# Where packing and spreading lie among the weight quads of an expert pair

## The reference

```python
def hier_moe(h, w_rg, b_rg, w_re, b_re, w_gate, w_up, w_down):
    ...
    gates = jnp.einsum('tk,tke->te', weight, jax.nn.one_hot(expert_id, N_EXPERTS, dtype=jnp.float32))
    y = jnp.zeros(hf.shape, jnp.float32)
    for e in range(N_EXPERTS):
        a = jax.nn.silu(hf @ w_gate[e]) * (hf @ w_up[e])
        y = y + gates[:, e:e + 1] * (a @ w_down[e])
```

## Time and profile before

| | |
|---|---|
| timed runs, median (lowest to highest) | 1892.45 us (1890.16 to 1892.65) |
| profiled execution | 1889.55 us |
| its span | 1887.5 us |
| mean granted TensorE clock | 0.963 |
| TensorE busy | 1793.5 us, 95% |
| VectorE, ScalarE busy | 506.8 us, 300.8 us |
| ring loads | 168 of 2 MB, median 9.1 us from issue to landing |

### The profile page before, as it was taken

One profiled execution on the slowest core, in us unless ns is written; L12 is line 12 of the kernel. 1 busy time (PEld: TensorE's weight loads), 2 busy tenths in 40 slices (PEclk: granted clock), 3 DMA queues, 4 the chain that ended last, 5 costly groups with the idle time before them and its releaser, 6 DMA issues.

```text
span 1887.5 us, 18695 instructions
## 1 busy us (share of the span) xinstructions
PE 1793.5 (95%) x7908; PEld 1127.3 (60%) x7908; DVE 506.8 (27%) x1066; ACT 300.8 (16%) x666; POOL 31.9 (2%) x34
## 2 busy tenths in 40 slices
PE   7999999999999899999899999999999998999996
PEld 5776676577666654444367666766667666544442
DVE  0027653441110311121200185534211013111122
ACT  2114220130120210001111142102211102100101
POOL 0000000000100000000000000000010000000000
PEclk9999999799999799999999999999999997999998
DMA  6323215553264279999813322255423551999992
GB/s 270 129 94 134 93 45 200 201 200 134 89 223 178 90 280 391 356 386 369 357 61 118 139 88 90 94 200 219 178 90 134 214 187 58 400 361 390 360 386 122
DMA packets 28681, 382.68 MB, mean 203 GB/s; under 512 B 3184, under 2 KB 3568, under 8 KB 3888
## 3 DMA queue, kind: packets, MB, share of 16 engines
q1 hardware_dynamic: 25040, 356.69, 48.9%
q0 software_dynamic: 3552, 24.71, 3.2%
HBM read 356.67 MB, written 24.71 MB: 202 GB/s over the span
## 4 chain that ended last, share of the span: by engine, by line
PE 87%; DVE 4%; ACT 4%; DVEq 2%; issue 1%; DMA 1%; ACTq 0%; POOL 0%; SPq 0%; POOLq 0%
PE psum L472 29%; PE psum L925 12%; PE psum L750 7%; PE psum L945 6%; PE psum L910 5%; PE psum L970 4%; PE psum L809 3%; PE psum L839 3%; PE psum L713 2%; PE psum L690 2%; PE psum L710 2%; DVE work L1455 2%; PE psum L700 2%; PE psum L479 1%; PE psum L877 1%
## 5 line engine op out<-in xcount | busy, mean ns | idle before, releaser
L472 PE MATMUL psum<-h,ring 128*128 128x320 f32 x1920 | 533.7, 438 | 7.7 <-DVE h L1380 6.3
L472 PEld LDWEIGHTS psum<-h,ring 128*128 128x128 f32 x1920 | 366.8, 192 | 164.9 <-issue 17.3
L925 PE MATMUL psum<-ring,work 128*64 128x512 f32 x1024 | 231.9, 597 | 1.6 <-ACT work L1325 1.4
L925 PEld LDWEIGHTS psum<-ring,work 128*64 128x64 f32 x1024 | 69.6, 137 | 137.3 <-issue 132.5
L750 PE MATMUL psum<-work,ring 128*128 128x320 f32 x512 | 138.3, 433 | 0.9 <-ACT work L1100 0.9
L472 PE MATMUL psum<-mem,ring 128*128 128x256 f32 x512 | 123.0, 395 | 4.0 <-ACT work L1100 4.0
L750 PEld LDWEIGHTS psum<-work,ring 128*128 128x128 f32 x512 | 97.1, 190 | 42.0 <-ACT work L1100 1.8
L945 PE MATMUL psum<-ring,work 128*64 128x512 f32 x512 | 115.1, 603 | 7.2 <-ACT work L1340 7.2
L472 PEld LDWEIGHTS psum<-mem,ring 128*128 128x128 f32 x512 | 98.5, 197 | 21.2 <-issue 7.1
L910 PEld LDWEIGHTS psum<-work 128*128 128x128 f32 x768 | 92.1, 199 | 25.0 <-issue 22.7
L910 PE MATMUL psum<-work 128*128 128x128 f32 x768 | 97.8, 286 | 1.4 <-ACT work L1313 1.4
(11 more groups left out here) (242 smaller groups left out, 1467.0 us busy)
## 6 DMA issues: line engine op xcount, KB each, us to landing
ring<-stream SPq DMA_DIRECT2D x168, 2048.0 KB, 9.1
st_out<-states_out POOLq DMA_DIRECT2D x18, 1024.0 KB, 9.2
mk_out<-k_mem POOLq DMA_DIRECT2D x2, 1024.0 KB, 6.1
mv_out<-work POOLq DMA_DIRECT2D x2, 1024.0 KB, 5.6
cst<-consts SPq DMA_DIRECT2D x1, 1456.0 KB, 22.3
x<-x_in SPq DMA_DIRECT2D x1, 1280.0 KB, 5.7
y_out<-h POOLq DMA_DIRECT2D x2, 640.0 KB, 3.2
mem<-mem_in SPq DMA_DIRECT2D x1, 1024.0 KB, 24.2
```

The source lines that it names most:

```text
L472: mm = pe.matmul(out, w[:, a:a + P], rhs[:, j, :], start=(j == 0), stop=(j == KD - 1))
L925: mm = pe.matmul(psum[ab * CAP:(ab + 1) * CAP, up, :], h_packed[:, p % 2, k, ab * CAP:(ab + 1) * CAP], w[:, a:a + BANK], start=(k == 0), s ...
```

## The change

The two fillers of the gate/up quads change places. Before, quads 0 and 1 were each followed by half of the spreading of pair p - 1, and quads 2 and 3 each by half of the packing of pair p + 1. After, quads 0 and 1 are followed by the packing, quads 2 and 3 by the spreading. Nothing else is changed; the programs of VectorE, ScalarE and SP stay as they are.

```diff
                     for m in range(4):
                         gate_up(p, m)
-                        if m < 2 and p > 0:
-                            spread(p - 1, range(4 * m, 4 * m + 4))
-                        if m >= 2 and p + 1 < PAIRS:
-                            pack(p + 1, m - 2)
+                        if m < 2 and p + 1 < PAIRS:
+                            pack(p + 1, m)
+                        if m >= 2 and p > 0:
+                            spread(p - 1, range(4 * m - 8, 4 * m - 4))
                     pe.wait_ge(s_hid, n_p + 1)
```

## The result

The changed kernel takes 1920.96 us (median, 1914.2 to 1923.73), the kernel before 1891.31 in the runs beside it: 1.0159 of before, 95% interval 1.0121 to 1.0197. The forecast was 1928.3 with a range from 1908 to 1948, so direction and range hold. The time was forecast 7 us too long. The growth was forecast at 38.7 us and measured at 29.7; the difference is smaller in the time because the forecast started from a profiled execution of 1889.55, which is 1.8 us under the median of before. The profiled execution took 1918.65 us, with a span of 1916.7 against 1887.5.

The account below looks back on a forecast made before the run. Expert stage paced by the order of matmuls, DMA queue close behind. 20.0 (chain) + 2.8 + 1.2 + 8.8 (ring) + 5.9 (clock) = +38.7 us on the profiled 1889.55 gave 1928.3 us, range 1908 to 1948.

Parts of the forecast that it names:

- chain, pairs 1 to 6: Between fourth quad and down, the multiplication waits for the last four adds: +1.42 us a pair, +17.0 for 12 pairs.
- chain, pair 0: Pair 0 has nothing to spread, so nothing follows its fourth quad before down: +1.65 us, twice +3.3.
- chain, pair 7: Pair 7's uncovered time before down goes from 2.81 to 2.64 us: -0.17, twice -0.3.
- ring, quads 0 and 1 in pairs 1 to 6: Late slot release delays weight loads: quad 0 waits add +2.8 us (0 to 17), quad 1 waits +1.2 (0 to 4).
- ring, pair 7: Without packing behind quads 0 and 1, loads of quads 1 and 2 come 2.9 and 1.5 us late: +8.8 (2 to 12).
- clock: TensorE's clock falls to 1.2 GHz behind 4.5 passages instead of 1, lengthening down by 1.69 us each: +5.9 us.
- The passage: From the fourth gate/up quad's end to down's start in pairs 1 to 6: 5.30 us instead of 4.11.
- The ring as pace (no change): Rival: weight loads set the pace at 0.94 busy, a longer chain costs nothing, time stays near 1890 us; chance 0.05.
- The faster case: Rival: SiLU, multiplication and transposes hide under the spreading, some -8 us, 1882 us; chance 0.03.
- The clock in most passages: Rival: the clock falls in most passages before down, say 12 times, +18.6 instead of +5.9, 1938 us; chance 0.12.
- loads late everywhere: Rival: loads for quad 0 land in 8.9 us as now, costing 17 us instead of 2.8, 1942.5 us; chance 0.10.

Follow-up runs that it names:

- banks_only: The changed kernel with hidden and gates transposed into banks 5 and 4, and ScalarE copying both packings before SiLU: 1924.25 us, 1.0161 of before.
- mult_first: As banks_only, with VectorE multiplying between the adds of chunks 3 and 4: 1912.28 us, 1.0116 of before.
- mid_pack: The kernel before, its second packing halved with the transposes of hidden between, ScalarE copying hidden before the packing: 1884.22 us, 0.9954 of before.
- fill_pair7: The changed kernel with twelve idle matmuls behind quad 0 and twelve behind quad 1 of pair 7: 1934.4 us, one run.
- ends_old: The changed kernel with pairs 0 and 7 put back in the old filler order: 1912.16 us, 1.0096 of before.
- release_early: The changed kernel with one small matmul behind quad 3 of pairs 1 to 7 that releases that quad's slot: 1921.78 us, 1.0156 of before.
- fill_pair0: The changed kernel with six idle matmuls behind quad 3 of pair 0: 1923.9 us, 1.0179 of before.
- mid_spread: As mult_first, with the transposes of hidden between the spreads of chunks 5 and 6, and the slot release of release_early: 1.0033 of before.

## Why the prediction held, step by step

| step | forecast, us | in the profiles, us |
|---|---|---|
| chain, pairs 1 to 6 | +17.0 | 12 x (34.87 - 33.58) = +15.5 |
| chain, pair 0 | +3.3 | 2 x (22.84 - 21.03) = +3.6 |
| chain, pair 7 | -0.3 | 2 x (5.18 - 2.66 - 2.83) = -0.6 |
| ring, quads 0 and 1 in pairs 1 to 6 | +2.8 + 1.2 | +2.2 - 0.5 = +1.7 |
| ring, pair 7 | +8.8 | 3.7 + 4.8 = +8.5 |
| clock | +5.9 | 2 x 1.69 = +3.4 |
| sum | +38.7 | +32.1, the stages show +32.2 |

For pair 0 the row takes the time from its first gate/up matmul to its down. The growth is 1.81 us, a little more than the 1.65 read from the passage alone.

**The passage.** The mechanism is the one forecast, and banks_only and mult_first settle it. The term was 0.12 us too long for a pair: the multiplication starts at 756.19 while the last add, from 755.25 on with 1.03 for two, ends at 756.28. The sum had the one start 0.02 after the other's end. Among VectorE's own instructions the hand-over is negative, -0.09.

One reading of the kernel before was not whole. The prediction leaves the 1.22 us behind the packing to ScalarE and calls the transposes covered by the packing. In before's timeline of TensorE the transposes (L479) fill 0.93 us of them, and only 0.47 is idle:

```profile
790.06 0.93 PE L479 MATMUL psum<-cst,work 128*128 128x128 f32 x7
791.46 7.09 PE L945 MATMUL psum<-ring,work 128*64 128x512 f32 x32 [0.47 <-ACT work L1340]
```

The sum does not suffer, for it takes the passage whole. But it is why mid_pack, which covers this idle time, gains 0.36 us for a passage and not 1.2.

**Ring, pairs 1 to 6.** The load for quad 0 fits, as forecast, with the excess of single loads on top (four periods above 34.87 in layer 2, the largest by 1.15, one in layer 1 by 0.34). The first period of layer 1 holds a further 0.15 us. The 2.8 us were a little high, and the 1.2 us for quad 1 were not needed: no regular wait shows there.

**Ring, pair 7.** Forecast 4.4 us for each layer, found 3.7 and 4.8 (last periods of 32.77 and 35.56 against 29.03 without waits, and 1.69 of the second is the clock). The split within is not as forecast: in layer 1 TensorE waits 1.88 for quad 1 and 1.63 for quad 2, where 2.9 and 1.5 were forecast, and in layer 2 it waits for quad 0 too (0.71, 1.66, 2.02). fill_pair7 shows that the waits need the missing filler. But the prediction has before's spreading cover them, and it does not once the release is late: ends_old, with that spreading in place, keeps 1.9 and 1.4 us. An earlier release alone, in release_early, took away 1.2 of the 8.5. The old fillers and the early release together were not tried.

**The clock.** This is the term that was most mis-sized. I took one fall in four for the 14 passages with spreading, from the single fall at a bare passage. None of them had one. The falls came behind pair 0 in both layers, and one in pair 7 of layer 2 behind a ring wait; before had one, so two more, 3.4 us for 5.9. And a fall costs less than its 1.69 where the next load would be late anyway (fill_pair0).

**The span.** The stages grew by 32.2 us, the span by 29.2: the untouched rest was 3.0 us shorter in this execution, within what it varies by.

The chain, the ring and the clock were all forecast too high, by 1.5, 2.6 and 2.5 us, and the shorter rest adds to it; nothing offset them, and the range was wide enough.

**The rivals.** The ring as pace (no change) is refuted by the periods, and by mid_pack's and mid_spread's, which are shorter than before's. The faster case rested on another order on VectorE. mid_spread has such an order, with the transposes in other banks and between the spreads besides, and its period of 33.17 shows that the idea can be had for pairs 1 to 6, while pairs 0 and 7 took it back. The clock in most passages and loads late everywhere did not occur.

## What to carry to other kernels

A filler is no filler if its own consumer stands ahead of the critical instruction on another engine's program: before moving work under a wait, list for each engine what that work puts in front of the instruction that ends the wait. Cutting a filler in two and issuing the short dependent step in the middle gave more than any choice between fillers. At the ends of a pipelined loop, where one filler doesn't exist, weigh the prefetch as well: two quads without filler, behind a load that started late, cost as much here as half of the main effect.

## What the runs showed of the hardware that I had not expected

A passage of 2.83 us with only seven transposes in it was followed by the clock's lower level (1.2 GHz) in 14 of 22 cases, and passages up to 5.41 us with four matmuls of spreading in them in none of 124. Six idle matmuls in the bare passage kept the clock at 2.4 GHz (down 7.08 to 7.10 us in four of four), without any gain in time that could be measured.
